# Five norms of a kernel take the first 128 tokens first, and the stage behind each begins on them with x stationary; bias tiles are read backwards

## What is computed

```python
def _layer_norm(x, g, b):
    mu = jnp.mean(x, axis=-1, keepdims=True)
    var = jnp.mean(jnp.square(x - mu), axis=-1, keepdims=True)
    return (x - mu) * lax.rsqrt(var + LN_EPS) * g + b

def _swiglu(x, w1, w2):
    gt, up = jnp.split(x @ w1, 2, axis=-1)          # w1: 1024 x 5632
    return (jax.nn.silu(gt) * up) @ w2              # w2: 2816 x 1024

def first_block(x, ...):
    for l in range(DEPTH):                          # DEPTH = 2
        x = _layer_norm(DN_ALPHA * x + 0.5 * _swiglu(x, ffn1_w1[l], ffn1_w2[l]), ln1_g[l], ln1_b[l])
        mix = _token_mix(x, w_in[l], ..., rel_bias, ..., w_out[l])
        x = _layer_norm(DN_ALPHA * x + mix, ln2_g[l], ln2_b[l])
        x = _layer_norm(DN_ALPHA * x + 0.5 * _swiglu(x, ffn2_w1[l], ffn2_w2[l]), ln3_g[l], ln3_b[l])
    return x
```

## Time and profile before

| | us |
|---|---|
| median of 3 runs | 2813.97 (2812.84 to 2817.15) |
| the profiled execution | 2814.42 |
| its span (first to last instruction) | 2812.5 |
| TensorE busy in it | 2646.6 (94%) |
| VectorE busy | 1283.4 (46%) |
| ScalarE busy | 1059.1 (38%) |
| GpSimd busy | 74.7 (3%) |
| mean DMA rate | 247 GB/s |

### The profile page before, as it was taken

The page is one execution under the profiler, slowest core; times in us unless marked ns, Lnnn a source line. Parts: engine busy times, 40 slices in busy tenths (PEclk is TensorE's granted clock), DMA queues, the critical chain, the costliest instruction groups (busy, mean ns, idle before and its releaser), DMA issues.

```text
span 2812.5 us, 40269 instructions
## 1 busy us (share of the span) xinstructions
PE 2646.6 (94%) x16566; PEld 1952.4 (69%) x16566; DVE 1283.4 (46%) x2353; ACT 1059.1 (38%) x1748; POOL 74.7 (3%) x30
## 2 busy tenths in 40 slices
PE   8999999999999999999989899989988999998996
PEld 8988988899898988889888754433336864443433
DVE  5565554755756565475677651111116653111112
ACT  4444563444444465344457641111114442111110
POOL 0001000100100100010010000000000000000000
PEclk9999999999999999999999999999999999999999
DMA  9645633555463853446353289999997149999997
GB/s 309 219 118 157 214 97 114 196 200 191 155 209 108 224 168 106 150 156 211 114 172 129 91 330 416 421 421 421 421 420 227 61 169 377 420 421 421 421 421 294
DMA packets 315366, 695.37 MB, mean 247 GB/s; under 512 B 58224, under 2 KB 243440, under 8 KB 266032
## 3 DMA queue, kind: packets, MB, share of 16 engines
q1 hardware_dynamic: 312000, 682.09, 66.1%
q10 hardware_dynamic: 3184, 10.69, 1.2%
HBM read 691.65 MB, written 1.08 MB: 246 GB/s over the span
## 4 chain that ended last, share of the span: by engine, by line
PE 65%; DMA 17%; DVE 10%; ACT 5%; issue 2%; SPq 1%; ACTq 0%; DVEq 0%
PE ps L295 26%; PE ps L2630 8%; PE ps L827 7%; DMA slots_over_xT<-in_moe_w_gate 6%; DMA ring<-in_moe_w_gate 6%; DMA moe_slots<-in_moe_w_gate 5%; PE ps L2680 4%; PE ps L1605 3%; PE ps L1645 3%; DVE weight_parts L226 3%; PE ps L334 2%; PE ps L306 2%; PE ps L2566 2%; ACT weight_parts L218 1%; SPq L2521 1%
## 5 line engine op out<-in xcount | busy, mean ns | idle before, releaser
L295 PE MATMUL ps<-xT_upper,weight_parts 128*128 128x256 f32 (+1 forms) x4656 | 844.9, 285 | 17.4 <-DVE arena L2241 7.1
L226 DVE TENSOR_TENSOR weight_parts<-ring,weight_parts 128x1024 fp32r<-128x1024 f32 x479 | 612.3, 1281 | 492.0 <-ACT weight_parts L218 491.4
L295 PEld LDWEIGHTS ps<-xT_upper,weight_parts 128*128 128x128 f32 (+1 forms) x4656 | 718.2, 189 | 41.3 <-DVE weight_parts L226 14.4
L218 ACT ACTIVATE weight_parts<-ring 128x1024 fp32r<-128x1024 f32 x479 | 504.1, 1055 | 533.8 <-PE ps L295 318.9
L295 PE MATMUL ps<-xT_lower,weight_parts 128*128 128x256 f32 (+1 forms) x2328 | 650.5, 283 | 1.9 <-DVE xT_lower L988 1.5
L295 PEld LDWEIGHTS ps<-xT_lower,weight_parts 128*128 128x128 f32 (+1 forms) x2328 | 438.2, 190 | 3.6 <-DVE xT_lower L988 2.8
L2630 PE MATMUL ps<-ring,bias_tiles 128*64 128x512 f32 x1024 | 241.8, 597 | 23.6 <-DMA ring<-in_moe_w_gate 12.2
L2919 DVE TENSOR_TENSOR arena<-ps,arena 128x512 f32<-128x512 f32 x32 | 22.1, 692 | 467.6 <-ACT arena L2794 467.5
L827 PE MATMUL ps<-weight_parts,hidden_upper 128*128 128x512 f32 x704 | 218.3, 391 | 4.5 <-DVE hidden_lower L880 4.5
L2794 ACT ACTIVATE arena<-ps 128x512 f32<-128x512 f32 x32 | 19.1, 598 | 490.0 <-PE ps L2630 490.0
L2630 PEld LDWEIGHTS ps<-ring,bias_tiles 128*64 128x64 f32 x1024 | 78.0, 137 | 178.9 <-issue 129.1
(11 more groups left out here) (336 smaller groups left out, 3196.6 us busy)
## 6 DMA issues: line engine op xcount, KB each, us to landing
ring<-in_ffn_w SPq DMA_DIRECT2D x132, 1024.0 KB, 5.2
ring<-in_moe_w_up SPq DMA_DIRECT2D x64, 1024.0 KB, 26.3
ring<-in_moe_w_gate SPq DMA_DIRECT2D x64, 1024.0 KB, 26.3
ring<-in_moe_w_down SPq DMA_DIRECT2D x64, 1024.0 KB, 26.6
moe_slots<-in_moe_w_up SPq DMA_DIRECT2D x48, 1024.0 KB, 26.4
moe_slots<-in_moe_w_down SPq DMA_DIRECT2D x40, 1024.0 KB, 25.9
slots_over_xT<-in_moe_w_gate SPq DMA_DIRECT2D x32, 1024.0 KB, 27.3
moe_slots<-in_moe_w_gate SPq DMA_DIRECT2D x32, 1024.0 KB, 26.2
```

The source lines that it names most:

```text
L218: act.activation(self.part(n, 0), cut(self.stream.slot(pos)), ACT.Copy).then_inc(self.upper_done, 1)
L226: dve.tensor_tensor(self.part(n, 1), cut(self.stream.slot(pos)), self.part(n, 0).bitcast(F32), ALU.subtract).then_inc(self.split, 1)
L295: m = pe.matmul(out[0:rows, :], w[of_w][:, k, :], c.xTp[of_x][:, k, :], start=(at == 0), stop=(at == len(steps) - 1))
```

## The change

- **A norm with `first`** (norms 1 to 5; norm 6 is as before). VectorE and ScalarE do all of token tile 0 before tile 1: VectorE normalises the first column half of a tile, ScalarE the second; ScalarE takes the first four blocks out of PSUM, VectorE the last four; then the parts. TensorE transposes tile 0, then does the products of the next stage's first four units for tile 0 in two pairs, with the transposes of tile 1 between them. One `keep_clock` of 512 columns goes before and one after the first transposes, and the 1024 columns at the end are gone.
- **x stationary** (`token_unit`, L382 in the new kernel): the first four units are `depth` units, 4 blocks by 256 columns. For each token tile 12 matmuls of 256 columns. The next stage does its tile 1 first of all.
- **Room for them**: three of the four units lie beside the ring of three (`units_beside_*`, in free stretches of the arena), and are split at the end of the stage before, by the `following` loops. The first feed-forward stage has no norm before it and keeps its four first units in the ring.
- **Feed-forward**: the first chunk's hidden values arise with tokens on the partitions. They are multiplied there (L1023) and turned by four transposes (L917), and their parts are taken out of PSUM (L1027). Chunk 1's four units of w1 come before chunk 0's w2 units, and its second pair behind the transposes. Plans and the stream's order follow. GpSimd waits for `U[6]`, the seventh unit.
- **Mixer**: the `vc` tiles are the first ones; the last tiles are now keys, which ScalarE copies.
- **Bias**: the table is stored in the other direction and already scaled; the flip stage, its matrix and its load are gone; `bias_back` reads a tile with step -1. The compressed branch's reads go from step 16 to step -16.

```diff
+def token_unit(c, pe, n, j, t, out, arrived, start, stop):
...
+    w = c.units.both(n)
+    c.units.ready(pe, n)
+    steps = [(k, of) for k in range(4) for of in PARTS[0:2]] + [(k, PARTS[2]) for k in range(4)]
+    for at, (k, (of_w, of_x)) in enumerate(steps):
+        if at in (0, 8):
+            ready = (c.xT_hi, c.x_parts)[of_x]
+            pe.wait_ge(ready.sem, ready.at(arrived + 2 * t + j))
+        m = pe.matmul(out, c.xTp[of_x][:, 4 * j + k, t * P:(t + 1) * P], w[of_w][:, k, :],
+                      start=(start and at == 0), stop=(stop and at == len(steps) - 1))
+    return m
...
+def bias_back(c, h, first, n):
...
+    return window(c.E[:, :], h * S + S - 1 - first, [[-1, n]])
...
-def flip_bias_stage(c):
...
+            def turn_first():
...
+                for t in range(TT):
+                    pe.wait_ge(c.h0_rows.sem, c.h0_rows.at(t + 1))
+                    for j in range(2):
+                        m = pe.transpose(turned(t)[:, j, :], h0[:, t, j * P:(j + 1) * P], c.ident[:, :])
+                    m.then_inc(c.h0_ps.sem, c.h0_ps.one())
...
-            for n in range(CHUNKS):
+            if ahead:
+                for i in range(FIRST):
+                    first(pe, 1, i, AFTER_NORM).then_inc(c.units.done, 1)
+            else:
+                for i in range(FIRST):
+                    m = first(pe, 0, i, AFTER_NORM)
+                    if i == FIRST - 1:
+                        m.then_inc(c.first_rows.sem, c.first_rows.one())
+                    first(pe, 1, i, AFTER_NORM).then_inc(c.units.done, 1)
+            hidden(1, 0)
+            turn_first()
+            hidden(1, 1)
+            for n in range(CHUNKS - 1):
+                if n >= 2:
+                    for half in range(2):
+                        hidden(n, half)
                 for half in range(2):
-                    hidden(n, half)
-                if n < CHUNKS - 1:
-                    for half in range(2):
-                        for t in range(TT):
-                            down(n, half, t)
+                    for t in range(TT):
+                        down(n, half, t)
+            for half in range(2):
+                hidden(CHUNKS - 1, half)
...
+            def first_rows(t):
+                dve.wait_ge(c.sg_full.sem, c.sg_full.at(t + 1))
+                dve.tensor_tensor(h0[:, t, :], ps[:, t, S:2 * S], sg[t][:, :], ALU.mult).then_inc(c.h0_rows.sem, c.h0_rows.one())
...
+            def first_lower(t):
+                dve.wait_ge(c.h0_hi.sem, c.h0_hi.at(t + 1))
+                dve.tensor_tensor(h0_parts[1][:, :, t * P:(t + 1) * P], turned(t), h0_parts[0][:, :, t * P:(t + 1) * P].bitcast(F32),
+                                  ALU.subtract).then_inc(c.h0_full.sem, c.h0_full.one())
...
+            for i, n_ in enumerate(U):
+                if i == FIRST - 1:
+                    if not ahead:
+                        first_rows(0)
+                    first_rows(1)
...
+                    if (n, j) == (1, 0):
+                        for t in range(TT):
+                            first_lower(t)
+                if i < len(U) - 2:
+                    c.units.lower(dve, c.units.after(n_))
+                if i == len(U) - 6:
+                    for n in following[0:2]:
+                        c.units.lower(dve, n)
+                if i == len(U) - 4:
+                    for n in following[2:]:
+                        c.units.lower(dve, n)
...
+        if first:
+            for h in range(2):
+                summed(0, h)
+                spread_of(0, h)
+            summed(1, 0)
+            scales(0)
+            normed(0)
+            spread_of(1, 0)
+            summed(1, 1)
+            raw_last(0)
+            spread_of(1, 1)
+            lower_part(0, 0)
+            scales(1)
+            normed(1)
+            lower_part(0, 1)
+            raw_last(1)
+            lower_part(1, 0)
+            lower_part(1, 1)
...
+        if first:
+            for t in range(TT):
+                if t:
+                    deviation(t)
+                normed(t, (1,))
+                raw_first(t)
+                upper_part(t, 0)
+                upper_part(t, 1)
+            for n in lead:
+                c.units.upper(act, n)
...
+        if first:
+            keep_clock(c, pe, CLOCK_ROWS[0])
+            turned_rows(0)
+            keep_clock(c, pe, CLOCK_ROWS[1])
+            for i in range(2):
+                first(pe, 0, i, IN_NORM)
+            turned_rows(1)
+            for i in range(2, FIRST):
+                m = first(pe, 0, i, IN_NORM)
+            m.then_inc(c.first_rows.sem, c.first_rows.one())
...
-                        dve.tensor_tensor_reduce(part(b["s"][n % 2][h], slot), part(ps[:, h, :], slot), c.E[:, at:at + SLOTS_AT[slot][1]],
+                        dve.tensor_tensor_reduce(part(b["s"][n % 2][h], slot), part(ps[:, h, :], slot), bias_back(c, p.bias[h], slot * P, SLOTS_AT[slot][1]),
```

More of the change, by code:

```diff
@@ L208, in both, with ready @@
         return [self.part(n, which) for which in range(2)]
+    def ready(self, eng, n):
+        if self.all[n][3] is None:
+            eng.wait_ge(self.split, self.order[n] + 1)
+        else:
+            eng.wait_ge(self.beside_split, self.order[n] + 1)
     def upper(self, act, n):
@@ L301, in value_unit @@
     w = c.units.both(units[j])
-    pe.wait_ge(c.units.split, units[j] + 1)
+    c.units.ready(pe, units[j])
     for t in range(TT):
@@ L330, in row_products @@
     w = c.units.both(n)
-    pe.wait_ge(c.units.split, n + 1)
+    c.units.ready(pe, n)
     for half in halves:
@@ L775, in __init__, with hidden @@
             down = s.add(row_piece(w2, n * CHUNK))
-            self.units += [c.units.add(pos, *column_unit(j), last=(j == 1)) for j in range(2) for pos in (gate, up)]
-            self.units += [c.units.add(down, *row_unit(j), last=(j == 1)) for j in range(2)]
+            self.units += columns(gate, up) + rows(down)
         self.end = len(s.loads)
-def ffn_stage(c, plan, load_norm, load_first=None):
+    def hidden(self, n, half, side):
+        return self.units[(4 if n == 1 else 6 * n) + 2 * half + side]
@@ L1097, in finish_rows @@
         if later:
-            pool.wait_ge(c.units.split, later)
+            c.units.ready(pool, later)
         pool.wait_ge(c.norm_loaded.sem, c.rows_pending)
@@ L1686, in keep_gate @@
                 if m < 21:
-                    c.units.upper(act, n + UNITS)
+                    c.units.upper(act, c.units.after(n))
                 act.wait_ge(c.units.done, n + 1)
@@ L1721, in _ @@
             for m in range(21, 24):
-                c.units.upper(act, plan.gate[m] + UNITS)
+                c.units.upper(act, c.units.after(plan.gate[m]))
             for q in range(4):
@@ L1815, in _ @@
                 while split < 21 and 2 * split + 1 <= 3 * n - 1:
-                    c.units.lower(dve, plan.gate[split] + UNITS)
+                    c.units.lower(dve, c.units.after(plan.gate[split]))
                     split += 1
@@ L2228, in ahead @@
             def ahead(n):
-                c.units.lower(dve, n + UNITS)
+                c.units.lower(dve, c.units.after(n))
             def conv(n):
```

432 lines of the change are left out of this document (287 added, 145 removed).

## The result

The changed kernel takes 2793.36 us in the median of 4 runs (2790.42 to 2796.82), the kernel before 2813.4 beside it (2810.27 to 2817.15): 0.9923 of the time, 95% interval 0.9911 to 0.9936. The prediction was 2794.5. The sum was right to 1.1 us, but not its terms: the largest was too favourable, three were too unfavourable, and two losses were missing. The profiled execution is the slowest of the four, 2796.82, its span 2795.0.

The account below looks back on a forecast made before the run. TensorE, busy 94% of the span, was taken as the bound in the first block. Terms 24.9+1.3+0.8-1.9-1.65-3.9 = 19.5 off 2814.4 gave 2794.9, or 2794.5 against the median; range 2787 to 2805, the forecast's own 2790 to 2800.

Parts of the forecast that it names:

- Norms: Norms 1 to 5: TensorE's time without products falls, saving 14.0 at norm 1, 5.3 at 3 and 4, 5.6 at 2 and 5.
- GpSimd: Three feed-forward stages: GpSimd from U[6] delays VectorE's splits, TensorE waits 2.1 in place of 0.8 each; -3.9, bounds 0 and -9.
- Splits ahead: Last chunk of ffn1, ffn2 and second ffn1: three more VectorE splits delay the last hidden tile, 0.55 each, -1.65.
- Into the heads: Start of scores: ScalarE copies the last tile, so VectorE's first biased scores come 0.65 earlier, twice; +1.3, bounds 0 and 2.2.
- Start: Kernel start: the first unit waits for x of tile 0 only, not both; half of 1.55 taken, +0.8.
- First hidden rows: Four feed-forward stages: four added transposes each at 0.116, -1.9; row operations covered by 5.7 us of chunk 1's products.
- Backward reading: Bias additions (L1742), read with step -1: no cost, 0; bounds 0 and a doubling of all 64 operations a layer.
- rival 4: Backward reading costs double in L1742: slower, 2834.5; chance 0.04, and 0.04 for half that price, 2814.5.
- GpSimd in the mixer stands at the same units as before: 0: Mixer: GpSimd's operations begin at unchanged units, so no gain or loss, 0.
- the second: Rival, no new waits: splits get through between GpSimd's operations and the tail's 0.55 is hidden; 5.55 back, 2789.5; chance 0.13.
- The third: Rival, split norm isn't shorter because VectorE releases parts late; only flip and its waits go, 6 gained, 2808.4; chance 0.07.
- The first: Rival, the clock falls more often: five more stretches at the lower level, 1.7 us each, 2803; chance 0.12.

Follow-up runs that it names:

- Experiment 2: Changed kernel with ScalarE's wait for the constants moved from the head of its norm list to behind the first root: 2784.63 us, 0.9892.
- Experiments 6: Experiment 5's kernel with GpSimd's four operations in the three feed-forward stages beginning at U[11] in place of U[6]: 2774.71 us, 0.9857.
- 7: Changed kernel with GpSimd scaling one column of x and not 1024, so its result is not the program's: 2786.37 us, 0.9908.
- experiment 4: Experiment 2's kernel with GpSimd scaling rows later in the mixer, from the unit of tile 11 of 15 on: 2781.85 us, 0.9881.
- experiment 3: Kernel before with the bias part alone: table stored the other way and scaled, read with step -1, no flip stage: 2806.07 us, 0.9968.
- experiment 8: Changed kernel without the two pieces of 512 columns of zeros in norms 1 to 5: 2803.53 us, 0.9957.
- 5: Experiment 4's kernel with GpSimd beginning one unit earlier behind norm 6, at dt+5 in place of dt+6: 2778.74 us, 0.9864.
- experiments 1: The changed kernel as it is, run again beside the kernel before: 2796.72 us, 0.993.

## Why the prediction was right in its sum and wrong in its terms

- **Norms, 24.9 forecast.** By the prediction's own count (length less 5.7 of products) norm 1 gives 18.98-5.8 = 13.2, norms 3 and 4 1.8 each, norms 2 and 5 8.5-6.7 = 1.8 each: 20.4. The step that failed is "then VectorE normalises its half (0.55) by 202.05 and ScalarE its own by 202.4": it takes the root to come with the statistics. The load that the earlier trace rows did not show moved behind them. Experiment 2 shows it: with the load early the chain of the prediction holds to 0.1 us at norm 3, and norms 2 and 5 take 11.15 where it had 11.4. The error was to cost only instructions that the change adds or moves by name, and not a load whose place follows from a wait put ahead of it.
- **Norm 6, not in the sum.** Its code is as before, but it shares that wait: 0.9 lost.
- **GpSimd, -3.9 forecast.** Measured waits are 0.41 and 0.33, 0.39 and 0.31, 0.41 and 0.32 in place of 1.3 and 0.75: 0.7 a stage, as before. Place and number of the waits were right, the size was not (and the prediction's own T+13.0 less T+11.8 is 1.2, not 1.3). TensorE could start behind the split of `U[8]` at 716.36; T is 704.1 (5.7 of products behind 698.40), so that is T+12.3 and not T+13.0. The step that failed is "Walking the list with 2.4 us for a GpSimd operation": the walk is 0.7 too long by there. VectorE's rows show where it grew: the split of `U[7]` ended at 710.41, T+6.3 and not T+6.6, the hidden tile at 712.95, T+8.85 and not T+9.4, and the first lower parts at 713.61, T+9.5 and not T+10.2. Experiments 6 and 7 show the stage's true loss by it, 1.3 us, restarts included; what it was in the kernel before by that count no run shows.
- **Splits ahead, -1.65 forecast.** Waits for the last hidden tile are 1.29, 1.1 before: -0.2 each. The step "which ends at 700.95, where the last hidden tile began at 700.41" takes 8.32 us for six splits and a hidden tile; they took 7.97 (672.68 to 680.65), since a split of 1.22 is followed by the next after 1.14 (VectorE, then TensorE, in ffn2's last chunk):

```profile
672.68 1.23 DVE L271 TENSOR_TENSOR weight_parts<-ring,weight_parts 128x1024 fp32r<-128x1024 f32 x1 [1.61 <-ACT weight_parts L260]
...
680.65 0.42 DVE L1043 TENSOR_TENSOR hidden_upper<-ps,silu 128x256 fp32r<-128x256 f32 x1
```

```profile
682.00 0.70 PE L932 MATMUL ps<-weight_parts,hidden_upper 128*128 128x512 f32 x2 [1.29 <-DVE hidden_lower L1047]
```

- **Into the heads, +1.3 forecast, bound 2.2.** Measured 2.8, above the bound. From the last product ahead of the scores to the third set of scores it was 13.06 us in each layer and is 11.68 now: 1.4 a layer. Layer 1 before, and now:

```profile
318.65 0.28 PE L1605 MATMUL ps<-xT_lower,weight_parts 128*128 128x256 f32 x1
...
331.71 0.92 PE L1532 MATMUL ps<-arena 64*128 64x256 f32 x8
```

```profile
303.42 0.28 PE L1880 MATMUL ps<-xT_lower,weight_parts 128*128 128x256 f32 x1
...
315.10 0.92 PE L1807 MATMUL ps<-arena 64*128 64x256 f32 x8
```

The waits tell another story: in layer 1 that of 1.79 at 330.91 (L1585) has no counterpart. But in that execution the lower clock lies just ahead of it,

```profile
306.80:310.10 3.30, 3.30 (x16) 2.90 (x17) 3.16 (x17) 1.91 (x10) 0.00 (x0) 0.50 0.05 16
```

and took as long as the wait would have. In experiment 4, without the lower clock there, the wait stands (1.47), and the distance is 11.67 all the same. So 9.7 against 7.6 is mostly an effect of where the lower clock fell: the changed kernel's second trace has 6.1 in that row. The step that failed is "I take 0.65 twice": the gain per layer was 1.4.
- **Start, +0.8 forecast.** The waits 1.55 and 0.43 became one of 1.21: 0.8.
- **First hidden rows, -1.9.** Their cover held: no wait of TensorE for them stands in the table.
- **Backward reading, 0.** 421 and 286 ns, as forecast; rival 4 is out, by experiment 3 too. Worked out from what the Trainium skill, SBUF — State Buffer, section "Door 1: The DMA port swizzle", says of lines of 16 bytes, the term was 0 as well; the trace agrees with that.
- **Behind norm 6, not in the sum.** 1.75 us of waiting became 3.37: -1.6. (From norm 6's first zeros to the next wait behind these, of 1.07 and 1.06, it is 44.73 before and 47.26 now, 2.5 more: these 1.6 and norm 6's 0.9.) "GpSimd in the mixer stands at the same units as before: 0" looked at the numbers of units, not at what `ready` means; in the mixer the two waits of 1.8 stayed as they were, here they grew.

The measured terms: 20.4-0.9+0-0.5+2.8+0.8-1.9-1.6 = 19.1, against 20.0 and 18.3 measured. The forecast met the time by luck: -4.5 in the norms, -2.5 where nothing was forecast, +3.9, +1.1 and +1.5 nearly cancel. Nor do the terms hold stage by stage. Lengths of the traces (each from a norm's first zeros), and what the terms give:

| from | before | changed | changed, second trace | shorter by | by the terms |
|---|---|---|---|---|---|
| the start | 201.5 | 201.0 | 202.1 | 0.5, -0.6 | 0.1 |
| norm 1, with mixer | 308.5 | 290.9 | 292.4 | 17.6, 16.1 | 14.6 |
| norm 2, with ffn2 | 196.7 | 195.1 | 195.0 | 1.6, 1.7 | 1.2 |
| norm 3, with ffn1 | 195.9 | 194.3 | 194.3 | 1.6, 1.6 | 1.1 |
| norm 4, with mixer | 297.0 | 297.0 | 292.4 | 0.0, 4.6 | 3.2 |
| norm 5, with ffn2 | 196.7 | 195.0 | 195.0 | 1.8, 1.7 | 1.4 |
| norm 6 to the end | 1416.3 | 1421.9 | 1423.6 | -5.6, -7.3 | -2.5 |

In the second mixer one trace of the changed kernel gained nothing and the other 4.6 us: the first has four stretches at the lower clock there (from 924.5, 1081.5, 1091.8 and 1102.0), the second and the kernel before two. Why each feed-forward stage gained about 0.4 more than its terms no run shows.

Of the rivals, the second came close: by its terms 5.55 come back, and 5.05 did (3.9 at GpSimd, 1.15 at the splits), though neither all waits nor the tail's are gone. The third is out: norm 3 is shorter by 1.8, not by nothing. The first didn't occur (no stretch at the lower clock in any of the five norms, and up to norm 6 six such stretches in each of the two traces, four in the second one of the changed kernel), but experiment 8 shows its mechanism at work as soon as the zeros are gone: "no single wait exceeds 1.3" was wrong (1.66 at norm 2, 1.82 at norm 5), and waits of 1.70 and 1.91 close together were enough, without any of 2.92.

## What to carry to other kernels

When a list of ScalarE gets a wait ahead of a root, look where the table load comes to stand: here one line was worth 1.0 us at each norm, and moving it gave 6.5 us, more than the new norm order saved at norms 3 and 4 together (3.6). Put GpSimd's work on SBUF where VectorE has only weight splits and room, and check each place again when the meaning of a wait's number changes; four edits (experiments 2, 4, 5 and 6) took a gain of 18 to 20 us to 40 (2774.71 against 2815.08). Between the traces of experiments 1 and 6, 5.7 of 23.4 us lie behind the last zeros, where no edit was made, so some 18 are theirs. And a sum that comes out right is no proof of its terms: compare wait by wait, and check each wait that vanished against the distance between the same two instructions, since a lower clock just ahead of a wait hides it.

## What the runs showed of the hardware

- A wait of TensorE of 0.39 us cost 0.66 in starts, and two that came to 0.7 cost 1.35 a stage. Here the price of a wait was the distance of starts around it less the pace, not the bracketed idle time.
- Two pieces of zeros of 512 columns kept the granted clock at 1.00 in the five norms; without them, with waits of 1.70 and 1.91 at norm 3, it fell to 0.50 in all five (experiment 8).
- GpSimd held up VectorE's cast from SBUF to SBUF, which has one input (2.26 us in place of 0.22), and did not hold up operations that read PSUM: L2585 took 0.42 beside it. The prediction counted "only operations with two inputs in SBUF as blocked", which is too narrow. The Trainium skill, SBUF — State Buffer, section "Who interferes with whom", counts copies and casts in a two-port mode among those that take the ports that VectorE shares with GpSimd. The trace shows that this cast was held up; which mode it ran in no row shows.
- A table load is 1.28 us, and the root follows at once (686.12+1.28 = 687.40, root at 687.41). The Trainium skill, ScalarE: Activation LUTs, section "What ACT_TABLE_LOAD costs", gives about 1.28 us for the load and 1.38 more for a drain at every switch. The trace shows the first alone, on an engine that had idled 4.74 us, and also between busy neighbours: in ffn1 behind norm 3 a rounding ends at 699.96, the load takes 699.97 to 701.25, and the next operation starts at 701.27. There the measurement decides.
- Reading a float32 operand with step -1 costs VectorE the same 421 ns for 256 elements as reading it forwards.
